# Norms and transposes of two output projections issued block by block between the units, feed-forward weight buffers swapped, and the final norm joined to each block's sums

## The chip, the cores and the metric

One core of one Trainium2 chip runs the whole program. The metric is the device time in microseconds of one execution. A core has TensorE (matmuls), VectorE (DVE), ScalarE (ACT) and GpSimd (POOL), each with a queue of its own worked off in order, and SyncE (SP), whose queue issues all the DMAs here. The engines are coupled by semaphores that the kernel writes out by hand.

## What is computed

Two transformer blocks on 1024 tokens of width 1024, in float32. The part that matters here is the end of each block:

```python
# first block
x = x + gate * (merged @ w_o)
x = rmsnorm(x, final_g)
# second block
h = rmsnorm(x, g_mix_pre);  proj = h @ w_in + b_in        # pool branch, attention branch, two gates
mix = merged @ w_out
x = x + rmsnorm(mix, g_mix_post)
h2 = rmsnorm(x, g_mlp_pre)
ff = square(relu(h2 @ w_up)) @ w_down                     # width 4096
x = x + rmsnorm(ff, g_mlp_post)
# rmsnorm(x, g) = x / sqrt(mean(x^2) + eps) * g, over the 1024 features of a token
```

## The kernel before

**Precision and units.** Every float32 operand of a projection is split into a high and a low part (`act_hi`, `act_lo`, `w_hi`, `w_lo`), and a product is three matmuls per 128 rows of depth. A unit is one PSUM bank (128 x 512) and takes 24 matmuls for a depth of 1024. `plan()` writes out one list of all units; unit number n uses bank n mod 4 (`acc`), and the semaphores `acc_ready` and `acc_free[0..3]` count units and evacuated banks, so the order of the list is the order in which TensorE and all evacuating engines work. The weights come in chunks of 8 pieces of 128 x 512: SP loads a piece into one of four `raw` slots, GpSimd casts it (L858) and subtracts (L860, `split_piece`) into one of two halves (slots) of `w_hi` and `w_lo`. A chunk's pieces may be written when the chunk two before is finished. SP's `prefetch` issues the loads of the next chunk's pieces during the current chunk's units.

**Output projections.** `wo` (first block) and `w2` (second) each have 16 units: first all eight token blocks B of the left column half (h = 0), then all eight of the right half (h = 1). VectorE evacuates each into the token-major buffer `tokT` (`evac_out`, L1459, L1461, and for `wo` an addition of x, L1465). After a block's right half ScalarE takes a mean square and a root (`mean_square_root`, L1080, L1082), VectorE scales (`norm_one`, L1470, L1471; for `w2` also the addition of the residual `x1`, L1476), ScalarE takes the mean square of that (`norm_second`), and VectorE writes the twice normed block to one of two buffers `xn` (`norm_two`, L1482, L1485). TensorE transposes it, two units of four 128 x 128 transposes per block (`turn_norm`, `turn`, L1685), named `ht` for the first block and `mt` for the second; ScalarE copies the high part out of PSUM (`split_hi`, L904) and VectorE subtracts for the low part (L1504). All turned units stand in the list behind the last unit of the projection. The next projection waits for the evacuation of the last of them, `wait_evac(pe, ("ht", 7, 1))`. What follows is `pl` (8 units) and `q` after `ht`, and the feed-forward part after `mt`.

**SP around it.** During the right half SP issues for each block the load of what is to be added (L737, L787), the store of a finished block to `x1_d` or `x2_d` (L742, L789), and the prefetches. The loads of the feed-forward weights follow behind the last two `x2_d` stores.

**Feed-forward.** The hidden width is done in NJ = 16 slices of 256. The order on TensorE is up(0), up(1), down(0), up(2), down(1), ... up(15), down(14), down(15). An `up` is 4 units of 24 matmuls (L1829), a `down` 16 units of 6 (L1842). The `up` weights lie in `w[:, 0, 0:4]`, the `down` weights in `w[:, 0, 4:8]`, the hidden activations (`hid`) in `w[:, 1]`. ScalarE takes Relu out of PSUM, VectorE multiplies by PSUM for the square, ScalarE copies the high part, VectorE subtracts. The `down` units are added into `tokT` by VectorE (L1612). GpSimd's `mlp_split(region, n0, ld, free)` waits for unit number `free` and then splits four pieces.

**End.** After the last `down`, VectorE runs `norm_one(2, B)` for the eight blocks; ScalarE's mean squares go along with the sums. SP refills the two `res` buffers with rows of `x2` (L817), each when the addition two blocks before is done, and stores the output rows (L819, L822).

Of the kernel before, what the change touches and what calls it, by code (L numbers as in the profile page):

```python
# [18 lines left out]
F32 = mybir.dt.float32  # L19
# [28 lines left out]
def plan():  # L48
# [3 lines left out]
    def chunk(key, us):  # L52
        chunks.append(key)
        units.extend(us)
        last[len(chunks) - 1] = [u for u in us if u[0] not in ("qt", "kt")][-1]
# [74 lines left out]
    chunk(("w2", 1), t_units("w2", 1))  # L130
    units.extend(("mt", B, h) for B in range(NB) for h in range(2))
# [37 lines left out]
def build(nc, A, out):  # L169
# [3 lines left out]
    M0 = len(units)  # L173
# [7 lines left out]
    with ExitStack() as ctx:  # L181
# [137 lines left out]
        rel, out_st = sem("rel"), sem("out_st")  # L319
# [127 lines left out]
        up_w = [w[:, 0, 0:4, :].rearrange("p a n -> p (a n)").rearrange("p (k n) -> p k n", k=KT)  # L447
                for w in (w_hi, w_lo)]
        down_w = [w[:, 0, 4:8, :].rearrange("p a n -> p (a n)").rearrange("p (k n) -> p k n", k=2)
                  for w in (w_hi, w_lo)]  # L450
# [33 lines left out]
        def _(sp):  # L484
# [291 lines left out]

            wait_evac(sp, ("yb", 7, 1))
# [17 lines left out]
            def mlp_pieces(src, j, before):  # L795

                for p in range(4):
                    sp.wait_ge(w_ready, before + p)
                    dst = raw[:, p, :].rearrange("p (k n) -> p k n", k=2) if src is up_src else raw[:, p, :]
                    sp.dma_start(dst, src(j, p)).then_inc(raw_ld[p], 16)  # L800

            mlp_pieces(up_src, 0, NP0 - 3)
# [24 lines left out]
        def _(pool):  # L827
# [54 lines left out]
            mlp_split(0, NP0, 0, U[chunk_last[len(chunks) - 2]] + 1)  # L882
            mlp_split(0, NP0 + 4, 1, M0 + 4)
            mlp_split(4, NP0 + 8, 2, M0 + 4)
            with pool.Fori(2, NJ) as k:

                mlp_split(0, NP0 + 8 * k - 4, 2 * k - 1, M0 + 20 * k - 32)
                mlp_split(4, NP0 + 8 * k, 2 * k, M0 + 20 * k - 16)
            mlp_split(4, NP0 + 8 * NJ - 4, 2 * NJ - 1, M0 + 20 * NJ - 16)
# [6 lines left out]
        def _(act):  # L896
# [191 lines left out]

            def normalise(r, name):
                for B in range(NB + 1):  # L1090
                    if B < NB:
                        if r == 0:
                            act.wait_ge(n_x[0], NB + B + 1)
                        else:
                            wait_evac(act, ("w2", B, 1))
                        mean_square_root(r, B, 0, n_s1[r])
                    if B >= 1:
                        norm_second(r, B - 1)
                for B in range(NB):
                    for h in range(2):  # L1100
                        wait_unit(act, (name, B, h))
                        split_hi((name, 2 * B + h), act_hi[:, 4 * h:4 * h + 4, P * B:P * B + P],
                                 bank((name, B, h)).rearrange("p (k s) -> p k s", k=4))
# [4 lines left out]
            for u in unit_range(("pl", 0, 0), ("pl", 3, 1)):  # L1108
                wait_unit(act, u)
# [34 lines left out]
            def mlp_relu(k, i, n0, before):  # L1144

                act.wait_ge(acc_ready, n0 + i + 1)
                if before is not None:
                    act.wait_ge(acc_free[i], before)
                nc.scalar.activation(relu[i], acc[i], ACT.Relu).then_inc(rel, 1)

            def mlp_hi(k, i, par, freed, down_done):
# [4 lines left out]
                nc.scalar.activation(hid[0][:, par, i // 2, HALF * (i % 2):HALF * (i % 2) + HALF], sq[i],  # L1156
# [9 lines left out]
            mlp_up(0, 0, M0, None, M4 + 1, None)  # L1166
# [12 lines left out]
        def _(dve):  # L1179
# [307 lines left out]

            def normalise(r, name):
# [3 lines left out]
                for B in range(NB + 2):  # L1492
                    if B < NB:
                        evac_out(r, B, 1, NB + B)
                    if 1 <= B <= NB:
                        norm_one(r, B - 1)
                    if 2 <= B < 4:
                        norm_two(r, B - 2)
                for B in range(NB):
                    for h in range(2):  # L1500
                        u = (name, B, h)
                        dve.wait_ge(hi_done, SPLIT[(name, 2 * B + h)])
                        cols = slice(P * B, P * B + P)
                        nc.vector.tensor_tensor(act_lo[:, 4 * h:4 * h + 4, cols],  # L1504
                                                bank(u).rearrange("p (k s) -> p k s", k=4),
                                                act_hi[:, 4 * h:4 * h + 4, cols].bitcast(F32), ALU.subtract
                                                ).then_inc(free_of(u), 1)
                    if B + 2 < NB:
# [382 lines left out]
```

## Time and profile before

| | |
|---|---|
| time, median of 3 runs | 2987.16 us |
| lowest and highest | 2985.3 and 2987.48 us |
| span of the profiled execution, core 0 | 2985.3 us, mean granted TensorE clock 0.958 |
| that execution's own time beside its span | 2985.3 us, the lowest run, agrees with the span to the digit shown; nothing is known to lie around it |
| busy: TensorE, VectorE, GpSimd, ScalarE | 93%, 46%, 30%, 21% of the span |
| DMA | 236.11 MB, mean 79 GB/s |

TensorE's two clock levels are 2.4 GHz (granted clock 1.00) and 1.2 GHz (0.50); values between are mixtures over a stretch. The chain that ended last is made of TensorE for 87% of the span, VectorE for 7%, DMA for 3%.

### The profile page before, as it was taken

To read this page: it belongs to the slowest core of one execution; us is meant where nothing else is said; L and a number is where in the kernel's file an instruction comes from. 1 tells how busy PE (TensorE), PEld (TensorE's weight loads), DVE (VectorE), ACT (ScalarE), POOL (GpSimd) and SP (SyncE) were. 2 spreads that over 40 slices of the span, in tenths; PEclk is the share of its full clock that TensorE was granted. 3 is DMA by queue.
4 is the path that set the end of the run, shared out by engine and by line. 5 is a ranking of instruction groups with operands and counts; after the bars stand their busy time and mean duration, and the time that the engine had idled before them with its cause. 6 is when DMAs were issued, how large, how long until landed. Compare 5 with 4: busy or idle time off the path is not lost.

```text
span 2985.3 us, 33951 instructions
## 1 busy us (share of the span) xinstructions
PE 2778.3 (93%) x12436; PEld 2214.1 (74%) x12436; DVE 1387.5 (46%) x2577; ACT 631.0 (21%) x1495; POOL 883.6 (30%) x862
## 2 busy tenths in 40 slices
PE   6799999999999998959898899998988999999995
PEld 2487778977799776738686777777767888888884
DVE  1411346977668675671543612224363334434435
ACT  3212222122311233440122022230141100110111
POOL 0541213323142322313343412214213433333330
PEclk8899999999999999979998999999989999999997
DMA  5410112112221222533332121214241111111112
GB/s 170 127 53 27 59 48 74 58 55 78 73 77 53 69 86 92 187 132 120 113 125 71 36 75 60 64 59 174 78 127 43 52 48 46 53 42 56 42 63 99
DMA packets 155597, 236.11 MB, mean 79 GB/s; under 512 B 24764, under 2 KB 69564, under 8 KB 155464
## 3 DMA queue, kind: packets, MB, share of 16 engines
q1 hardware_dynamic: 155464, 234.35, 24.3%
q8 instruction: 82, 1.34, 0.2%
q14 instruction: 51, 0.42, 0.0%
HBM read 181.65 MB, written 52.64 MB: 78 GB/s over the span
## 4 chain that ended last, share of the span: by engine, by line
PE 87%; DVE 7%; DMA 3%; issue 1%; POOL 1%; ACT 1%; SPq 0%; POOLq 0%; DVEq 0%; ACTq 0%
PE ps L1673 50%; PE ps L1829 12%; PE ps L1842 12%; PE ps L1731 5%; PE ps L1741 3%; PE ps L1755 3%; PE ps L1685 2%; PE ps L1702 2%; DVE act_lo L1196 1%; DVE scr L1283 1%; DMA small<-st_d 1%; DVE act_lo L1504 1%; DMA scr<-x_d 1%; POOL w_lo L860 1%; DMA scr<-in_x 0%
## 5 line engine op out<-in xcount | busy, mean ns | idle before, releaser
L858 POOL CAST w_hi<-raw 128x512 fp32r<-128x512 f32 x416 | 311.5, 749 | 2012.4 <-DMA raw<-in_w_in 932.1
L1673 PE MATMUL ps<-act_hi,w_hi 128*128 128x512 f32 x1344 | 558.2, 415 | 50.4 <-DVE act_lo L1196 46.5
L860 POOL TENSOR_TENSOR w_lo<-raw,w_hi 128x512 fp32r<-128x512 f32 x416 | 580.2, 1395 | 33.3
L1673 PE MATMUL ps<-act_lo,w_hi 128*128 128x512 f32 x1344 | 533.3, 397 | 0.0
L1673 PE MATMUL ps<-act_hi,w_lo 128*128 128x512 f32 x1344 | 531.2, 395 | 0.0
L1283 DVE SCALAR_TENSOR_TENSOR scr<-scr,small 128x512 f32<-128x512 f32 x480 | 420.6, 876 | 11.5
L1673 PE MATMUL ps<-w_hi,act_hi 128*128 128x512 f32 (+1 forms) x960 | 386.8, 403 | 6.7 <-DVE act_lo L1196 6.6
L1673 PE MATMUL ps<-w_lo,act_hi 128*128 128x512 f32 (+1 forms) x960 | 376.4, 392 | 0.0
L1673 PE MATMUL ps<-w_hi,act_lo 128*128 128x512 f32 (+1 forms) x960 | 376.3, 392 | 0.0
L1673 PEld LDWEIGHTS ps<-act_hi,w_hi 128*128 128x128 f32 x1344 | 257.2, 191 | 104.5 <-issue 56.5
L1673 PEld LDWEIGHTS ps<-act_lo,w_hi 128*128 128x128 f32 x1344 | 256.0, 190 | 57.6
L1673 PEld LDWEIGHTS ps<-act_hi,w_lo 128*128 128x128 f32 x1344 | 257.5, 192 | 45.6 <-issue 0.2
L1673 PEld LDWEIGHTS ps<-w_hi,act_hi 128*128 128x128 f32 x960 | 233.6, 243 | 31.8 <-issue 12.5
L1673 PEld LDWEIGHTS ps<-w_hi,act_lo 128*128 128x128 f32 x960 | 234.0, 244 | 20.9
L1673 PEld LDWEIGHTS ps<-w_lo,act_hi 128*128 128x128 f32 x960 | 234.6, 244 | 19.3
L1000 ACT ACTIVATE scr<-scr,stat 128x256 f32<-128x256 f32 (+1 forms) x256 | 118.6, 463 | 512.5 <-DVE stat L1306 510.8
L1612 DVE TENSOR_TENSOR big<-big,ps 128x512 f32<-128x512 f32 x240 | 161.3, 685 | 135.0 <-PE ps L1842 135.0
L1829 PE MATMUL ps<-act_hi,w_hi 128*128 128x512 f32 x512 | 201.3, 393 | 10.1 <-POOL w_lo L860 8.7
L1842 PE MATMUL ps<-w_hi 128*128 128x512 f32 x512 | 200.7, 392 | 7.9 <-POOL w_lo L860 7.9
L1829 PE MATMUL ps<-act_hi,w_lo 128*128 128x512 f32 x512 | 200.8, 392 | 0.0
L1829 PE MATMUL ps<-act_lo,w_hi 128*128 128x512 f32 x512 | 200.8, 392 | 0.0
L1842 PE MATMUL ps<-w_lo,w_hi 128*128 128x512 f32 x512 | 200.5, 392 | 0.0
(166 smaller groups left out, 3111.4 us busy)
## 6 DMA issues: line engine op xcount, KB each, us to landing
raw<-in_w_in SPq DMA_DIRECT2D x176, 256.0 KB, 3.1
raw<-in_w_up SPq DMA_DIRECT2D x64, 256.0 KB, 2.6
raw<-in_w_down SPq DMA_DIRECT2D x64, 256.0 KB, 2.6
vreg<-in_w_ada SPq DMA_DIRECT2D x48, 256.0 KB, 3.5
raw<-in_w_in SPq DMA_DIRECT2D x72, 128.0 KB, 2.2
x_d<-big SPq DMA_DIRECT2D x16, 512.0 KB, 3.0
scr<-x_d SPq DMA_DIRECT2D x16, 512.0 KB, 4.4
o_d<-scr SPq DMA_DIRECT2D x48, 128.0 KB, 2.0
```

The costliest lines, as they stand in the source:

```text
L858: pool.tensor_copy(dhi, src).then_inc(w_hi_done, 1)
L860: pool.tensor_tensor(dlo, src, dhi.bitcast(F32), ALU.subtract).then_inc(w_ready, 1)
L1000: nc.scalar.activation(prob[a % 2][:, 0:n], prob[a % 2][:, 0:n], ACT.Exp, scale=-1.0, bias=stat[:, B, h:h + 1], accum_out=stat[:, B, 8 + h ...
L1283: nc.vector.scalar_tensor_tensor(ca, u_in[:, j:j + HALF], w[:, j:j + 1], ca, ALU.mult, ALU.add).then_inc(tap, 1)
L1612: ins = nc.vector.tensor_tensor(dst, dst, acc[i % ACC], ALU.add)
L1673: ins = nc.tensor.matmul(out_, lhs, rhs, start=(m == 0), stop=(m == 3 * nk - 1))
L1685: ins = nc.tensor.transpose(bank(u)[:, P * i:P * i + P], src, ident[:, :])
L1731: nc.tensor.matmul(ps_s[a % 2][:, 0:n], qT[rows, pair, P * B:P * B + P], keys, start=True, stop=True).then_inc(scores, 1)
L1741: ins = nc.tensor.transpose(ps_t[:, P * i:P * i + P], prob[a % 2][:, P * i:P * i + P], ident[:, :])
L1755: ins = nc.tensor.matmul(ps_o[:, 0:HD], probT[a % 2][:, P * i:P * i + P], v, start=(i == 0), stop=(i == n // P - 1))
L1829: ins = nc.tensor.matmul(acc[i], up_w[b][:, k, P * t:P * t + P], act_p[a][:, k, HALF * h:HALF * h + HALF], start=(m == 0), stop=(m == 23))
L1842: ins = nc.tensor.matmul(acc[i % ACC], hid[a][:, par, k, P * B:P * B + P], down_w[b][:, k, HALF * h:HALF * h + HALF], start=(m == 0), stop ...
```

## The change

- The turned units of `ht` and `mt` move up in the list. From block 2 on, behind the right-half unit of block B stand the two turned units of block B - 2 (`normed`). Block 6 is turned after the first unit of what follows, block 7 after the second. `pl` is reordered for it: first the left token halves of two tiles with blocks 6 and 7 turned between, then the left halves of the other two, then the right halves. A left half needs only blocks 0 to 3, so the first `pl` unit waits for `("ht", 3, 1)` and the fifth for `("ht", 7, 1)`. The `mt` side does the same with up(0), whose four units become entries of the list (`up`, t, h) in the order left, left, right, right. All `up` groups take this order of tile and half.
- VectorE and ScalarE run in the order that this asks for: per block evacuate, `norm_two` of the block before, low halves of the block two before, `norm_one`; ScalarE: high halves of two blocks before, first mean square, second mean square.
- Weights: up(0) in region 0, the other `up` in region 4, `down` in region 0, except the last `down`, in region 4. Up(1) is split when `w2`'s left half is done (before: after up(0)), the last `down` after up(15) (before: after down(14)). The loads of the up(0) pieces are issued by SP at block 3 of the right half of `w2`.
- End: `mlp_last` adds the last `down` and scales block by block; the reciprocal and scaling of block B - 1 follow the two sums of block B. The addition of the residual goes to GpSimd. The loads, the stores and the two `res` buffers are as before.

```diff
@@ plan()
-    chunk(("wo", 1), t_units("wo", 1))
-    units.extend(("ht", B, h) for B in range(NB) for h in range(2))
-    chunk(("pl", 0), f_units("pl", range(4)))
+    def turned(name, B):
+        return [(name, B, h) for h in range(2)]
+    def normed(name, turns):
+        us = []
+        for B in range(NB):
+            us.append((name, B, 1))
+            us += turned(turns, B - 2) if B >= 2 else []
+        chunk((name, 1), us)
+    normed("wo", "ht")
+    chunk(("pl", 0), [("pl", 0, 0)] + turned("ht", 6) + [("pl", 1, 0)] + turned("ht", 7)
+          + [("pl", t, h) for h in range(2) for t in range(4)][2:])
...
-    chunk(("w2", 1), t_units("w2", 1))
-    units.extend(("mt", B, h) for B in range(NB) for h in range(2))
+    normed("w2", "mt")
+    units += [("up", 0, 0)] + turned("mt", 6) + [("up", 1, 0)] + turned("mt", 7) + [("up", 0, 1), ("up", 1, 1)]
@@ SP, right half of w2
+                        if B == 3:
+                            mlp_pieces(up_src, 0, NP0 - 3)
@@ GpSimd
-            mlp_split(0, NP0, 0, U[chunk_last[len(chunks) - 2]] + 1)
-            mlp_split(0, NP0 + 4, 1, M0 + 4)
-            mlp_split(4, NP0 + 8, 2, M0 + 4)
+            mlp_split(0, NP0, 0, U[chunk_last[last_chunk - 1]] + 1)
+            mlp_split(4, NP0 + 4, 1, U[chunk_last[last_chunk - 1]] + 1)
+            mlp_split(0, NP0 + 8, 2, M0 + 4)
...
-            mlp_split(4, NP0 + 8 * NJ - 4, 2 * NJ - 1, M0 + 20 * NJ - 16)
+            mlp_split(4, NP0 + 8 * NJ - 4, 2 * NJ - 1, M0 + 20 * NJ - 32)
+            for B in range(NB):
+                pool.wait_ge(n_scaled, B + 1)
+                pool.wait_ge(n_ld[2][B % 2], 16 * (B // 2 + 1))
+                pool.tensor_tensor(tokT[:, B, :], tokT[:, B, :], res[B % 2], ALU.add).then_inc(n_y[2], 1)
@@ ScalarE, normalise
                 for B in range(NB):
+                    if B >= 2:
+                        turned_hi(name, B - 2)
...
                     mean_square_root(r, B, 0, n_s1[r])
+                    norm_second(r, B)
@@ ScalarE, after normalise(1, "mt")
-            mlp_up(0, 0, M0, None, M4 + 1, None)
+            first_relu(0)
+            turned_hi("mt", 6)
+            first_relu(1)
+            turned_hi("mt", 7)
+            first_hi(0)
+            first_hi(1)
+            first_relu(2)
+            first_relu(3)
+            first_hi(2)
+            first_hi(3)
@@ VectorE, normalise
                 for B in range(NB):
                     evac_out(r, B, 0, B)
+                for B in range(NB):
+                    evac_out(r, B, 1, NB + B)
+                    if B >= 1:
+                        norm_two(r, B - 1)
+                    if B >= 2:
+                        turned_lo(name, B - 2)
+                    norm_one(r, B)
+                norm_two(r, NB - 1)
@@ VectorE, after normalise(1, "mt")
-            mlp_square(0, 0)
+            first_square(0)
+            turned_lo("mt", 6)
+            first_square(1)
+            turned_lo("mt", 7)
+            mlp_lo(0, 0, 0)
+            mlp_lo(0, 1, 0)
...
@@ VectorE, end
-            mlp_add(NJ - 1, M0 + 20 * NJ - 16, False, M4 + 5 * NJ - 4)
-            dve.wait_ge(bc_ld, 96)
-            for B in range(NB):
-                norm_one(2, B)
+            mlp_last(NJ - 1, M0 + 20 * NJ - 16, M4 + 5 * NJ - 4)
+            # in mlp_last, for B in range(NB + 1): the two sums of block B, then for block B - 1:
+                        dve.wait_ge(n_s1[2], B)
+                        link(nc.vector.reciprocal(r, r))
+                        nc.vector.scalar_tensor_tensor(tokT[:, B - 1, :], tokT[:, B - 1, :], r, bc[2][0],
++                                                       ALU.mult, ALU.mult).then_inc(n_scaled, 1)
```

## Rows read from the trace of the kernel before

**Rows 1.** The page: busy time, share of the span and instructions per engine.

```profile
PE 2778.3 (93%) x12436; PEld 2214.1 (74%) x12436; DVE 1387.5 (46%) x2577; ACT 631.0 (21%) x1495; POOL 883.6 (30%) x862
```

**Rows 2.** Stretches: length, busy time and instructions per engine, granted clock, DMA share, GB/s.

```profile
1572.30:1599.40 27.10, 13.51 (x64) 10.88 (x62) 23.74 (x34) 13.36 (x25) 18.20 (x14) 0.63 0.42 133
...
2207.50:2235.80 28.30, 13.55 (x64) 10.91 (x62) 25.10 (x35) 13.44 (x25) 10.66 (x8) 0.62 0.43 145
2235.80:2260.50 24.70, 24.61 (x96) 19.81 (x96) 3.27 (x6) 2.83 (x5) 0.00 (x0) 0.89 0.00 1
2260.50:2269.20 8.70, 0.05 (x1) 0.05 (x1) 3.05 (x3) 1.75 (x3) 8.21 (x9) 0.77 0.26 87
...
2923.50:2931.50 8.00, 0.12 (x2) 0.02 (x1) 0.69 (x1) 0.00 (x0) 7.31 (x8) 0.74 0.00 0
2931.50:2956.50 25.00, 24.93 (x96) 20.01 (x96) 10.36 (x16) 10.13 (x21) 0.00 (x0) 0.88 0.00 1
2956.50:2985.30 28.80, 0.00 (x0) 0.00 (x0) 21.32 (x25) 1.44 (x3) 0.00 (x0) 0.59 0.77 255
```

**Rows 3.** Chain of waits from 1500 us on: start, length, what.

```profile
1572.29 0.70 DVE big L1461
1573.02 0.70 DVE big L1465
...
1599.48 56.33 PE ps L1673 x240
...
2269.15 23.41 PE ps L1829 x96
...
2314.32 21.76 PE ps L1829 x96
```

**Rows 4.** Chain of waits in stage Z, turned units between projection units.

```profile
1247.27 0.87 PE ps L1685 x8
```

**Rows 5.** Stretches of stage Z, the transposes (L1685) alone: PE, PEld, clock, DMA.

```profile
1240.00:1280.00 40.00, 7.60 (x60) 6.67 (x60) 1.00 0.62 199
```

**Rows 6.** Timeline after the last w2 unit: start, length, engine, instruction, [idle before].

```profile
2207.53 0.69 DVE L1459 TENSOR_SCALAR big<-ps 128x512 f32<-128x512 f32 x1 [2.11 <-PE ps L1673]
...
2208.25 1.06 ACT L1080 ACTIVATE scr<-big 128x1024 f32<-128x1024 f32 x1 [1.32 <-DVE big L1459]
...
2209.43 0.29 ACT L1082 ACTIVATE stat<-stat,small 128x1 f32<-128x1 f32 x1
...
2210.98 1.28 DVE L1471 SCALAR_TENSOR_TENSOR big<-big,stat,vreg 128x1024 f32<-128x1024 f32 x1
...
2216.94 1.29 DVE L1485 SCALAR_TENSOR_TENSOR vreg<-big,stat,vreg 128x1024 f32<-128x1024 f32 x1
...
2218.14 1.28 DVE L1504 TENSOR_TENSOR act_lo<-ps,act_hi 128x512 fp32r<-128x512 f32 x2
...
2218.78 1.27 POOL L860 TENSOR_TENSOR w_lo<-raw,w_hi 128x512 fp32r<-128x512 f32 x1
...
2219.44 0.60 ACT L904 ACTIVATE act_hi<-ps 128x512 fp32r<-128x512 f32 x1 [2.46 <-PE ps L1685]
2219.53 1.60 DVE L1485 SCALAR_TENSOR_TENSOR scr<-big,stat,vreg 128x1024 f32<-128x1024 f32 x1
2219.99 1.61 POOL L858 CAST w_hi<-raw 128x512 fp32r<-128x512 f32 x1
```

**Rows 7.** Timeline of GpSimd at the end of `wo`.

```profile
1568.29 0.61 POOL L858 CAST w_hi<-raw 128x512 fp32r<-128x512 f32 x1 [2.77 <-DMA raw<-in_w_in]
1568.98 2.16 POOL L860 TENSOR_TENSOR w_lo<-raw,w_hi 128x512 fp32r<-128x512 f32 x1
```

**Rows 8.** Source view of L787, the loads of x1 rows under w2.

```profile
DMA to landing us min/median/max: 4.0/4.3/4.8
```

**Rows 9.** Source view of L817, the loads of x2 rows at the end.

```profile
DMA to landing us min/median/max: 3.5/5.0/5.8
```

**Rows 10.** Timeline of VectorE, its last instruction.

```profile
2981.00 1.22 DVE L1476 TENSOR_TENSOR big<-big,scr 128x1024 f32<-128x1024 f32 x1 [0.52 <-DMA scr<-x_d]
```

More of the change, by code:

```diff
@@ L54, in chunk @@
         units.extend(us)
-        last[len(chunks) - 1] = [u for u in us if u[0] not in ("qt", "kt")][-1]
+        last[len(chunks) - 1] = [u for u in us if u[0] not in ("qt", "kt", "ht", "mt")][-1]
     def f_units(name, tiles):
@@ L172, in build @@
     taps_after = tap_plan()
-    M0 = len(units)
+    M0 = len(units) - 4
     assert M0 % ACC == 0
@@ L445, in down_src, with mlp_w @@
             return w_down[bass.ds(j * FC + P * (p // 2), P), HALF * (p % 2):HALF * (p % 2) + HALF]
[L447 to L450, printed above, removed]
+        def mlp_w(region, nk):
+            return [w[:, 0, region:region + 4, :].rearrange("p a n -> p (a n)").rearrange("p (k n) -> p k n", k=nk)
+                    for w in (w_hi, w_lo)]
+        UPS = [("up", i % 2, i // 2) for i in range(4)]
         hid = [w[:, 1, :, :].rearrange("p a n -> p (a n)").rearrange("p (i t s) -> p i t s", i=2, t=2)
@@ L774, in _, with mlp_pieces @@
                 gate_load(i + 32, ("y2", 3), u, "g2p" if u[0] == "yp" else "g2a")
+            def mlp_pieces(src, j, before):
+                for p in range(4):
+                    sp.wait_ge(w_ready, before + p)
+                    dst = raw[:, p, :].rearrange("p (k n) -> p k n", k=2) if src is up_src else raw[:, p, :]
+                    sp.dma_start(dst, src(j, p)).then_inc(raw_ld[p], 16)
             wait_evac(sp, ("yb", 7, 1))
@@ L1486, in norm_two, with turned_lo @@
                                                bc[r][2 if r == 0 else 1], ALU.mult, ALU.mult).then_inc(n_xn[r], 1)
+            def turned_lo(name, B):
+                for h in range(2):
+                    u = (name, B, h)
+                    dve.wait_ge(hi_done, SPLIT[(name, 2 * B + h)])
+                    cols = slice(P * B, P * B + P)
+                    nc.vector.tensor_tensor(act_lo[:, 4 * h:4 * h + 4, cols],
+                                            bank(u).rearrange("p (k s) -> p k s", k=4),
+                                            act_hi[:, 4 * h:4 * h + 4, cols].bitcast(F32), ALU.subtract
+                                            ).then_inc(free_of(u), 1)
             def normalise(r, name):
@@ L1491, in normalise @@
                     evac_out(r, B, 0, B)
[L1492 to L1498, printed above, removed]
[L1499 to L1509 removed]
+                for B in range(NB):
+                    evac_out(r, B, 1, NB + B)
[5 more added lines that the diff above has]
+                norm_two(r, NB - 1)
             normalise(0, "ht")
+            turned_lo("ht", 6)
+            turned_lo("ht", 7)
             def pooling(t):
@@ L1816, in _, with up_unit @@
                 turn(("a2", B, 0), [yv[:, B, P * i:P * i + P] for i in range(4)])
-            for u in unit_range(("yp", 0, 0), ("w2", 7, 1)):
-                project(u)
-            turn_norm(1, "mt")
+            def up_unit(i, out_, region):
+                t, h = i % 2, i // 2
+                up_w = mlp_w(region, KT)
+                for m in range(24):
+                    k, (a, b) = m // 3, PARTS[m % 3]
+                    ins = nc.tensor.matmul(out_, up_w[b][:, k, P * t:P * t + P],
+                                           act_p[a][:, k, HALF * h:HALF * h + HALF],
+                                           start=(m == 0), stop=(m == 23))
+                ins.then_inc(acc_ready, 1)
+            for u in unit_range(("yp", 0, 0), ("up", 1, 1)):
+                if u[0] == "mt":
+                    turn_norm(1, u)
+                elif u[0] == "up":
+                    begin(u)
+                    pe.wait_ge(w_ready, NP0 + 4)
+                    wait_evac(pe, ("mt", 3 if u[2] == 0 else 7, 1))
+                    up_unit(UPS.index(u), bank(u), 0)
+                else:
+                    project(u)
             def up(bank_free, weights):
@@ L1824, in up, with down @@
                 for i in range(4):
-                    t, h = i // 2, i % 2
                     pe.wait_ge(acc_free[i], bank_free)
-                    for m in range(24):
-                        k, (a, b) = m // 3, PARTS[m % 3]
-                        ins = nc.tensor.matmul(acc[i], up_w[b][:, k, P * t:P * t + P],
-                                               act_p[a][:, k, HALF * h:HALF * h + HALF],
-                                               start=(m == 0), stop=(m == 23))
-                    ins.then_inc(acc_ready, 1)
-            def down(j, par, bank_free, weights):
+                    up_unit(i, acc[i], 4)
+            def down(j, par, bank_free, weights, region=0):
+                down_w = mlp_w(region, 2)
                 pe.wait_ge(w_ready, weights)
```

114 lines of the change are left out of this document (69 added, 45 removed).

## Prediction

> **What bounds the kernel now.** I read the page first: TensorE is busy 93% of the span [rows 1], so time is lost only where it stands still or runs at half clock. The chain of waits, cut to the two output projections and the end, shows such places, and a table of stretches gives their size [rows 2]. There are three.
>
> Place A, after the first output projection `wo`: 27.1 us in which TensorE has 64 transposes and nothing else, at a granted clock of 0.63, a mixture of its levels 1.2 and 2.4 GHz. From the last `wo` unit (evacuated at 1572.29) to the end of the 240 matmuls that follow it is 1655.8 - 1572.1 = 83.7 us [rows 3]. Place B, after `w2`: 28.3 us of the same, then the first `up` group in 24.7 us instead of the 21.76 us of a steady one, then 8.7 us in which only GpSimd works (the weights of the second `up` go where those of the first lie, so their split waits for its end), then 23.4 us for the second group. From 2207.3 to 2292.6 it is 85.2 us [rows 2, 3]. Place C, the end: 8.0 us wait for the split of the last `down` weights, 25.0 us for that `down` at clock 0.88, and 28.8 us of VectorE and DMA without one matmul. From 2923.6 to 2985.3 it is 61.7 us [rows 2]. Everything else on TensorE stays as it is.
>
> The span is 2985.30 us, and the fastest of the three runs shown is 2985.30 us, so nothing lies around the span; the median is 1.9 us above. The sum is made on the span and moved by 1.9 us.
>
> **Place A after the change.** The same 64 transposes are issued, now in sixteen turns of four between units of 24 matmuls. Stage Z of the kernel before does this already: eight transposes between two units take 0.87 us at full clock [rows 4, 5]. That makes 8 x 0.87 = 7.0 us. The 240 matmuls cost 240 x 21.76/96 = 54.4 us at full clock, against 56.33 [rows 3]. After: 61.4 us, if VectorE and ScalarE keep up. A block has 5.44 + 0.87 = 6.3 us. VectorE needs per block 1.4 to evacuate (two of 0.70 [rows 3]), 1.5 for the second scaling, 1.3 for two low halves, 1.5 for the first scaling [rows 6]: 5.7 us, and the ring of VectorE's scaling (1.5), ScalarE's mean square (1.5, from 2208.25 to 2209.72), the second scaling and the low halves is 5.8 us, under 6.3. The turns of block 7 come two units later than its data, so nothing waits. If GpSimd's splits add 0.3 to each of VectorE's three SBUF instructions, a block takes 6.6 us, and 8 x 0.3 us of lag fit into those two units. Gain 83.7 - 61.4 = 22.3 us, with 20 as the lower end. SP's queue: it issues the `x1` stores and the prefetch of the pieces for `q` in the old order, each behind a norm that comes no later than before; the `q` units are 50 us away, against 8 pieces of some 2.9 us (1.27 + 1.61 [rows 6]).
>
> **Place B after the change.** `w2` has an addition more (1.22 [rows 10]), and here the ring closes: first scaling with addition 2.7, ScalarE's mean square 1.5 (the next evacuation, 0.69, lies beside it), second scaling 1.5, low halves 1.3, together 7.0 us against 6.3 us of TensorE. The first norm of a block ends 6.9 us behind its unit at block 2 and 0.7 us later with each block: 10.4 at block 7. The mean square and the second scaling bring it to 13.5 us behind the last unit, and then VectorE has two squares and four low halves, 2 x 0.69 + 4 x 0.64 = 3.9, before it frees the last turned bank: 17.6 with the latencies. TensorE, with two turns, two `up` units and two turns more, could go on at 2 x 5.44 + 3 x 0.87 = 13.5. It waits 4.1 us. Until there it doesn't wait, since it needs of a block only what VectorE did one block before.
>
> GpSimd now splits the first `up` weights inside `w2`. The trace shows what it does to VectorE when both read SBUF: the scaling that starts 0.75 us after a split's subtraction takes 1.60 us instead of 1.29, and the cast behind it 1.61 us instead of 0.61 [rows 6, 7]. The two take turns. Eight GpSimd instructions cost VectorE nothing where they meet PSUM work, and at most 1.1 us each (a whole subtraction but its end), 8.8 us together. I take 1.5 us, near what four such meetings cost in the rows (4 x 0.3). TensorE's wait is then 5.6 us, bounds 2 and 13. The Trainium skill ("SBUF — State Buffer", SBUF: two separate sides) says that the pair of ports is an exclusive lock held for a whole instruction; the rows agree (1.27 + 1.28 without overlap), and by it the upper end would hold only if every instruction met its opposite.
>
> Weights: the first `up` pieces are loaded behind SP's block 3, and SP's wait there (the first norm of block 1) is fulfilled. They are 5 us of load and 8 to 12 us of split, done by block 6 or 7, before they are needed 7 us behind the last unit. The second ones wait on SP for the last norm and the last two `x2` stores: 10.4 + 0.9 + a load of 4 [rows 8] + a split of 7.5 (4 x 1.88) to 11.5 (4 x 2.88 [rows 6, 7]) = 23 to 27 us behind the last unit. They are needed at 17.6 + 2 x 5.44 = 28.5 us. So the 8.7 us go, at the price of a slack of 2 to 6 us only. After: 7.0 + 8 x 5.44 + 5.6 = 56.1 us; gain 85.2 - 56.1 = 29.1 us. ScalarE mixes Relu, Square, square root and Copy, between which the trace of before has no table load, so the mixing costs nothing.
>
> **Place C after the change.** The last `down` weights get the region that the last `up` has left, and are split under the `down` before: 8.0 us go, and with them the cold clock. `down` yields a block every 2.72 us. VectorE adds twice (1.3), scales (1.5), so it could do 2.9 us per block; what is new is that GpSimd adds the residual, and that two residual buffers are refilled behind it. No row shows GpSimd adding 1024 columns. The nearest is 512 columns in 1.27 us, so twice that at most, 2.5; a part of it is fixed, and I take 2.4. Its upper end is 4.3 us, twice the 2.16 us of a subtraction that met VectorE [rows 7]. The Trainium skill ("GPSIMD Engine Reference", 3.1 Elementwise) gives 4497 ns for 2048 columns; by that figure it would be about 2.3 us, and place C 0.7 us shorter. Two bounds on the cadence agree: taking turns with VectorE's scaling, 2.4 + 1.3 = 3.7 us; and the buffers, (2.4 + 4.8 + 0.1)/2 = 3.65 us with a load of 4.8 us, between the 4.3 us under `w2` and the 5.0 us of the tail [rows 8, 9]. The first addition can start 7.6 us into the `down` (four units, 5.44, an addition, a scaling). End: 7.6 + 7 x 3.65 + 2.4 + 3.1 (last addition to span end, as 2982.2 to 2985.3 [rows 10]) = 38.7 us. Gain 61.7 - 38.7 = 23.0 us. Bounds: with VectorE's cadence of 2.9 us it is 33 us and a gain of 28; with 4.3 us on GpSimd and turns of 5.4 us it is 53 us and a gain of 9. VectorE's instructions are late when GpSimd holds the port, but a `down` unit has four banks.
>
> **Sum.** 22.3 + 29.1 + 23.0 = 74.4 us: 2985.3 - 74.4 = 2910.9, moved by 1.9: 2912.8 us.
>
> **Rivals.** (1) *The end isn't won*: GpSimd's additions of 4.3 us set the cadence; 14 us less, 2927 us. For it: casts and subtractions that grew by 1.0 us in the rows; against it: they grew only when they met an SBUF instruction, once per block. Chance 0.13. (2) *VectorE falls behind in `w2`*, TensorE waits the full 13 us or more, and the second `up` weights, queued on SP behind the late norms, use up their slack: 8 to 12 us less, 2923 us. For it: the ring is already over the cadence; against it: the meetings in the rows cost 0.3. Chance 0.12. (3) *The clock falls under the mixed units.* Transposes alone ran at 0.63 in the gaps. If they pulled the clock down to 1.2 GHz under the sixteen units that have turns beside them, each would take 5.44 us more: 87 us, so 3000 us, slower than before; it decides from 14 such units on. Against it: stage Z has 60 transposes among its units at clock 1.00 [rows 5]. The Trainium skill ("TensorE: Matmul & The Clock Gate", Part 4: PE-mode transpose) states that transposes don't count as busy for the gate, which is the rule that speaks for this rival; the trace agrees for transposes alone. Chance 0.02. (4) *Better than forecast*: no meetings in `w2`, cadence of 2.9 us at the end: 85 us, 2902 us. Chance 0.12. The forecast itself, place by place within some 6 us: 0.60. That a part does nothing (weights still late) would cost 8 us and lies in the range: 0.01.
>
> Measurement tells this kernel from no change at about 0.2%, 6 us. The range of 2900 to 2930 us takes in the forecast and rivals 1, 2 and 4, and leaves out their far ends and rival 3. Faster 0.97, same 0.01, slower 0.02.
>
> **What would show it.** In the profile after: no stretch between `wo` and `pl` without matmuls, clock 0.97 or more there; between `w2` and `down` 56 us with one or two waits of TensorE for VectorE's low half of about 4 us in all, before the third `up` unit; no wait for GpSimd before the second `up` and the last `down`; GpSimd additions of 2.4 to 3.5 us, every 3.6 us, and a last chain of GpSimd, DMA load, GpSimd. Wrong would be a clock below 1 in the mixed stretches, `w_ready` waits, or additions over 4 us.

## The result, and the profile of the changed kernel

The changed kernel takes 2914.66 us (median of 4 runs, 2912.68 to 2915.22), the kernel before 2987.32 us (4 runs, 2985.3 to 2988.4): a ratio of 0.9756, 95% interval 0.9742 to 0.977. The forecast was 2912.8 us. The profiled execution took 2915.05 us with a span of 2912.9 us, so 2.15 us lie around the span. By that, the span of before (2985.30 us) belonged not to the run of 2985.3 us but to one that took some 2 us more (later runs of the same kernel show 1.8 us between the two, 2987.12 us with a span of 2985.3). The forecast said that nothing lies around the span and moved its sum by the 1.9 us between the median and the fastest run: that this is near the true distance is luck. Spans are compared with spans below, 2985.3 with 2912.9, 72.4 us apart where the forecast's sum had 74.4.

The page, part 1, after; it answers to [rows 1]:

```profile
PE 2759.7 (95%) x12436; PEld 2198.0 (75%) x12436; DVE 1386.1 (48%) x2569; ACT 627.4 (22%) x1495; POOL 897.2 (31%) x870
```

The same 12436 matmuls; TensorE is busy 18.6 us less, which is the cold clock that has gone, and the rest of the 72.4 us were gaps.

Stretches of the changed kernel, columns as in [rows 2]: place A; the mixed units of `w2`; its last two turns with two `up` units; the six `up` units behind; the last `down`; the end.

```profile
1572.30:1599.40 27.10, 27.10 (x133) 22.66 (x132) 12.31 (x19) 10.28 (x21) 13.25 (x15) 1.00 0.48 150
...
2103.00:2192.00 89.00, 88.21 (x404) 72.07 (x403) 40.74 (x55) 23.43 (x48) 25.55 (x24) 1.00 0.31 98
2192.00:2209.50 17.50, 15.05 (x73) 11.38 (x73) 14.80 (x23) 10.31 (x22) 2.65 (x4) 1.00 0.46 164
2209.50:2244.00 34.50, 34.48 (x145) 28.41 (x146) 9.20 (x11) 5.19 (x9) 14.00 (x13) 0.95 0.19 62
2875.08:2900.00 24.92, 21.93 (x97) 17.60 (x95) 21.93 (x27) 10.12 (x21) 11.96 (x5) 0.99 0.54 160
2900.00:2912.90 12.90, 0.00 (x0) 0.00 (x0) 7.37 (x7) 1.44 (x3) 7.03 (x3) 0.50 0.73 261
```

Against [rows 2]: the 27.1 us of place A that held 64 transposes at clock 0.63 now hold full work at 1.00. In place B two things are left: 17.5 us with 15.05 us of work, and a clock of 0.95 behind them. In place C only 12.9 us are left without a matmul, where it was 28.8.

**Place A**, chain of waits (start, length, what), answering to [rows 3]:

```profile
1571.79 4.54 PE ps L1748 x20
1576.33 0.87 PE ps L1760 x8
...
1589.90 43.57 PE ps L1748 x192
1633.47 0.44 PE ps L1760 x4
```

TensorE alone is on the chain, with two turns (eight transposes) in 0.87 us. The 240 matmuls end at 1633.47 instead of 1655.81: 22.3 us gained. From there to the start of `w2` the trace is 0.8 us longer than before.

**Place B**, from the last wait inside the first `w2` unit to the first `down`; before 2124.94 to 2292.56, 167.6 us. The chain after, in pieces:

```profile
2103.42 44.50 PE ps L1748 x195
...
2149.83 1.28 ACT L1100
...
2168.50 1.74 DVE vreg L1528
...
2171.54 1.49 DVE big L1514
2173.06 2.20 DVE big L1519
...
2186.46 1.30 DVE big L1514
...
2193.34 1.30 DVE big L1514
...
2208.18 1.21 DVE act_lo L1536 x2
2209.52 34.52 PE ps L1895 x144
```

It now takes 140.6 us: 27.0 gained, 29.1 forecast. (A row of the chain runs from one wait to the next, so the first one begins inside the first `w2` unit, where TensorE last waited.) From 2147.94 to 2209.52 the chain isn't TensorE's any more but the ring of VectorE and ScalarE: the first scaling (L1514) begins every 6.88 us (2186.46, 2193.34). The row of 1.28 us without a tile is a load of ScalarE's table ahead of the first square root. The last row has 144 matmuls in 34.52 us, where full clock makes 32.64.

**Place C**, from the last `down` (2875.08) to the end: 37.8 us instead of 61.7, 23.9 gained, 23.0 forecast. The chain ends as the forecast said, with an addition of GpSimd, the load of the last residual rows and GpSimd again:

```profile
2900.50 2.37 POOL big L907
...
2902.89 4.24 DMA scr<-x_d
```

That load lands at 2907.13, 0.3 us before VectorE's last scaling ends, so both hold the last addition back about equally. Timeline of the last blocks:

```profile
2900.35 1.27 DVE L1664 TENSOR_TENSOR big<-big,ps 128x512 f32<-128x512 f32 x2
2900.50 2.36 POOL L907 TENSOR_TENSOR big<-big,scr 128x1024 f32<-128x1024 f32 x1 [1.16 <-DVE big L1669]
...
2901.73 2.21 DVE L1669 SCALAR_TENSOR_TENSOR big<-big,stat,vreg 128x1024 f32<-128x1024 f32 x1
...
2904.02 2.34 POOL L907 TENSOR_TENSOR big<-big,scr 128x1024 f32<-128x1024 f32 x1 [1.16 <-DVE big L1669]
2904.05 3.39 DVE L1669 SCALAR_TENSOR_TENSOR big<-big,stat,vreg 128x1024 f32<-128x1024 f32 x1
2906.39 3.83 SPq L834 DMA_DIRECT2D out_y<-big  x2
2907.52 2.34 POOL L907 TENSOR_TENSOR big<-big,scr 128x1024 f32<-128x1024 f32 x1 [1.16 <-DVE big L1669]
```

GpSimd's additions take 2.34 us, and VectorE's scaling, 1.28 us alone, takes 2.21 and at last 3.39 us. Both of these scalings end 1.08 us behind the end of the addition that they met (2903.94 behind 2902.86, 2907.44 behind 2906.36), wherever they began. That is what taking turns looks like: nearly the whole scaling comes after the addition.

The sum: 22.3 + 27.0 + 23.9 - 0.8 = 72.4 us, the difference of the spans.

### The profile page after: what moved, and what is told of

It reads as the page before. It is cut to its first block, busy times and chain, and to the rows that moved or that the text cites. A ratio compares the mean times of both kernels' runs of the same rounds, so it can differ in the third digit from the quotient of the medians.

```text
span 2912.9 us, 33971 instructions
## 1 busy us (share of the span) xinstructions
PE 2759.7 (95%) x12436; PEld 2198.0 (75%) x12436; DVE 1386.1 (48%) x2569; ACT 627.4 (22%) x1495; POOL 897.2 (31%) x870
## 4 chain that ended last, share of the span: by engine, by line
PE 87%; DVE 8%; DMA 3%; ACT 1%; issue 1%; POOL 0%; SPq 0%; POOLq 0%; ACTq 0%; DVEq 0%
PE ps L1748 50%; PE ps L1895 12%; PE ps L1927 11%; PE ps L1806 5%; PE ps L1816 3%; PE ps L1830 3%; PE ps L1760 2%; PE ps L1777 2%; DVE act_lo L1239 1%; DVE scr L1326 1%; DMA small<-st_d 1%; DMA scr<-in_x 1%; DVE scr L1429 0%; DVE big L1669 0%; DVE big L1519 0%
## 5 line engine op out<-in xcount | busy, mean ns | idle before, releaser
L1748 PEld LDWEIGHTS ps<-w_lo,act_hi 128*128 128x128 f32 x960 | 234.4, 244 | 19.1
L1681 DVE TENSOR_TENSOR big<-big,ps 128x512 f32<-128x512 f32 x224 | 150.0, 684 | 112.5 <-PE ps L1927 112.5
```

The costliest lines, as they stand in the source:

```text
L1681: ins = nc.vector.tensor_tensor(dst, dst, acc[i % ACC], ALU.add)
L1748: ins = nc.tensor.matmul(out_, lhs, rhs, start=(m == 0), stop=(m == 3 * nk - 1))
```

## The experiments

All are the changed kernel with one edit each, except the last ones, which join several. The kernel before ran beside each group (medians 2987.79, 2988.2 and 2987.35 us); ratios are to it. What lies ahead of `w2` differs by some us from run to run with the same code (in the seven kernels that are alike up to `w2` the chain's `w2` row starts between 2100.83 and 2103.74), so effects under 4 us are read as lengths of stretches, in the one execution of each kernel that was profiled. These repeat: `changed_again`, the changed kernel once more, has 140.64 us in place B where the first had 140.62.

**1. Place A undone.** The first output projection goes back to all units and then all transposes, on every engine.

```diff
-    normed("wo", "ht")
+    chunk(("wo", 1), t_units("wo", 1))
+    units.extend(("ht", B, h) for B in range(NB) for h in range(2))
...
```

> The changed kernel with place A undone: all turned units of ht behind the last wo unit, pl in its old order, VectorE and ScalarE in the old order there; the rest as changed. Theory of the prediction (place A gives 22.3 us by itself, half of it idle time, the rest clock): 22 us slower than the changed kernel, about 2937 us. Rival (part of the gain at A is given back at the next place where TensorE waits for VectorE, the pooling or the yp load): under 18 us slower.

Measured: 2939.05 us, ratio 0.9831 [0.9815, 0.9848], span 2936.6, 23.7 us over the changed kernel's. From the last `wo` unit (1572.33) to the end of the 240 matmuls (1657.02) it is 84.7 us. Places B and C kept their lengths (140.6 and 37.9 us): the gain of place A is its own and isn't given back later. Of the 23.7 us, 1.2 are the 240 matmuls behind the gap, 57.50 us here and 56.33 in the kernel before: the clock behind the same gap wasn't quite the same.

**2. The two buffer swaps undone, one each.** GpSimd's split of the second `up` weights waits until the first `up` has been read, that of the last `down` weights until the `down` before has.

```diff
-            mlp_split(4, NP0 + 4, 1, U[chunk_last[last_chunk - 1]] + 1)
+            mlp_split(4, NP0 + 4, 1, M0 + 4)
```
```diff
-            mlp_split(4, NP0 + 8 * NJ - 4, 2 * NJ - 1, M0 + 20 * NJ - 32)
+            mlp_split(4, NP0 + 8 * NJ - 4, 2 * NJ - 1, M0 + 20 * NJ - 16)
```

> The changed kernel, but the split of the second up weights waits for the end of the first up again, though it has a region of its own. Theory: the 8.7 us wait of TensorE and about 1.7 us of half clock after it come back: 9 to 10.5 us slower than the changed kernel, about 2925 us. Rival (the region alone is worth it, or the split hides behind units): under 4 us slower.

> The changed kernel, but the split of the last down weights waits for the down before it again. Theory: 7.9 us wait and 3.2 us of half clock come back on TensorE, and since VectorE and GpSimd at the end follow TensorE only for the first blocks, the 3.2 us are partly hidden: 9 to 11 us slower, about 2925 us. Rival (the end is set by GpSimd and the loads alone, which can start early): under 5 us slower.

Measured: 2924.41 us (0.9788 [0.9772, 0.9805], span 2923.2) and 2926.04 us (0.9795 [0.9778, 0.9811], span 2923.4), 9.7 and 11.4 us over the changed kernel's median. Chain of the first:

```profile
2208.05 12.76 PE ps L1895 x48
...
2220.99 0.61 POOL w_hi L870
...
2229.47 24.83 PE ps L1895 x96
```

and of the second:

```profile
2874.63 0.04 POOLq L890
...
2881.16 1.27 POOL w_lo L872
...
2882.47 11.23 PE ps L1927 x36
```

The waits of before are back, 8.7 us and 7.8 us, and behind each TensorE loses 3.1 us more (24.83 instead of 21.76 us for 96 matmuls; 11.23 instead of 8.16 for 36): a swap is worth its wait and the clock behind it, some 11 us. In place B that makes 152.6 us, 11.9 over; the run's total shows 10.3, because its `w2` began 1.7 us earlier (2101.75 instead of 2103.42), which is within the scatter named above.

**3. The residual on VectorE.** GpSimd's eight additions at the end become eight of VectorE.

```diff
-                pool.tensor_tensor(tokT[:, B, :], tokT[:, B, :], res[B % 2], ALU.add).then_inc(n_y[2], 1)
...
+                        nc.vector.tensor_tensor(tokT[:, B - 1, :], tokT[:, B - 1, :], res[(B - 1) % 2], ALU.add
+                                                ).then_inc(n_y[2], 1)
```

> The changed kernel, but the residual at the end is added by VectorE behind its scaling, GpSimd does nothing there. Theory (in the changed kernel GpSimd's 2.4 us and VectorE's 1.2 us take turns, 3.57 us per block): VectorE alone needs two sums 1.27, scaling 1.45, addition 1.25, about 4.0 us per block, its last addition is 1.1 us shorter: 1 to 2.5 us slower than the changed kernel, about 2916.5 us. Rival (moving the addition to GpSimd was what gave the gain at the end): over 8 us slower. Second rival (the loads set the cadence in both): same within 1 us or faster.

Measured: 2913.75 us (0.9756 [0.974, 0.9772]), no change; the end takes 37.7 us instead of 37.8. A miss:

```profile
2898.04 1.29 DVE L1665 SCALAR_TENSOR_TENSOR big<-big,stat,vreg 128x1024 f32<-128x1024 f32 x1
...
2901.89 1.28 DVE L1665 SCALAR_TENSOR_TENSOR big<-big,stat,vreg 128x1024 f32<-128x1024 f32 x1
...
2904.54 1.28 DVE L1665 SCALAR_TENSOR_TENSOR big<-big,stat,vreg 128x1024 f32<-128x1024 f32 x1
2905.95 1.23 DVE L1668 TENSOR_TENSOR big<-big,scr 128x1024 f32<-128x1024 f32 x1
```

The cadence is worse as expected, 3.85 us (2898.04 to 2901.89) instead of 3.5 to 3.6. But the last scaling and addition take 1.28 + 1.23 us, where the changed kernel has 3.39 + 2.34. From the first scaling to the last it is 25.8 us instead of 22.7; from there to the end of the span 5.7 us instead of 8.9. What the blocks before lose, the last one gives back. The total is that of the expectation's second rival (the loads set the cadence), but not by its mechanism: VectorE works without a wait from 2878.8 to 2905.8, and only the last addition waits for its load, 0.1 us.

**4. VectorE adds only the last two residuals, and there are three residual buffers.** GpSimd keeps blocks 0 to 5.

```diff
-            for B in range(NB):
+            for B in range(6):
                 pool.wait_ge(n_scaled, B + 1)
-                pool.wait_ge(n_ld[2][B % 2], 16 * (B // 2 + 1))
+                pool.wait_ge(n_ld[2][B % 3], 16 * (B // 3 + 1))
...
```

> The changed kernel, but three residual buffers at the end, and VectorE adds the residual of the last two blocks. Theory (GpSimd and VectorE take turns, the loads are not what ends): VectorE's last scaling no longer waits 2 us for GpSimd, and the last addition takes 1.2 instead of 2.4 us: 1.5 to 2.5 us faster. Rival (the loads set the end): the third buffer gives 3 us or more. Second rival (the store and its 5 us set it): same within 0.5 us.

Measured: 2911.93 us (0.975 [0.9736, 0.9763]); the end takes 35.8 us, 2.0 less than the changed kernel's. And it tells which of the forecast's two bounds sets the cadence, for the loads are a block earlier here:

```profile
2892.97 2.27 DVE L1672 SCALAR_TENSOR_TENSOR big<-big,stat,vreg 128x1024 f32<-128x1024 f32 x1
...
2895.32 2.35 POOL L910 TENSOR_TENSOR big<-big,scr 128x1024 f32<-128x1024 f32 x1 [1.17 <-DVE big L1672]
...
2896.54 2.21 DVE L1672 SCALAR_TENSOR_TENSOR big<-big,stat,vreg 128x1024 f32<-128x1024 f32 x1
```

It is still 3.57 us (2892.97 to 2896.54), and the scaling again ends 1.08 us behind the addition (2898.75 behind 2897.67). GpSimd and VectorE taking turns set it; the third buffer did nothing for the cadence.

**5. The lag in `w2`: table, meetings, order.** Three edits, one each, against the 1.9 us that TensorE loses before its last `w2` unit and the 4.0 us behind it. `table_early`: a square root of one constant on ScalarE ahead of each `normalise`. `load_early`: SP issues the loads of the first `up` pieces four blocks of its loop earlier and so ahead of every wait for a norm; GpSimd splits them from 2142.3 to 2150.1, before the first scaling begins at 2151.3.

```diff
...
+            nc.scalar.activation(tiny[:, 35:36], epsc[:, 0:1], ACT.Sqrt)
             normalise(1, "mt")
```
```diff
-                        if B == 3:
-                            mlp_pieces(up_src, 0, NP0 - 3)
+                    elif B == 7:
+                        mlp_pieces(up_src, 0, NP0 - 3)
```

`ring_order`: the halves of an older block give way to the norm of the new one, on both engines.

```diff
-                    if B >= 2:
-                        turned_lo(name, B - 2)
                     norm_one(r, B)
+                    if B >= 2:
+                        turned_lo(name, B - 2)
...
```

> The changed kernel with one more square root of one column on ScalarE ahead of each normalise, so that the table load of 1.28 us lies under the left half. Theory (in w2 VectorE and ScalarE form a ring of 6.9 us per block against 6.3 us of TensorE, so every microsecond of delay at its start is paid by TensorE): 1.3 to 2.5 us faster than the changed kernel. Rival (there is slack at the start of the ring, or the loss at B is the half clock alone): same within 0.5 us.

> The changed kernel, but SP loads the first up pieces at the end of the left half of w2, so GpSimd splits them under blocks 0 and 1 instead of 2 to 4. Theory (the meetings at the SBUF ports cost VectorE 1.6 us of the ring): 1 to 2 us faster, less what blocks 0 and 1 pay. Rival (the meetings cost the same wherever they are): same within 0.5 us.

> The changed kernel, but per block ScalarE takes the first mean square before it copies the high halves, and VectorE makes norm_one before the low halves, so that these lie beside ScalarE's mean square. Theory (ring): the ring of w2 falls from 6.9 to about 6.3 us, TensorE waits only for the third up unit, about 2 us, and the half clock behind it goes: 3 to 6 us faster, about 2910 us. Rival (VectorE's sum of work of 6.2 us per block is the limit, not the ring): under 1.5 us faster.

Measured: 2913.37 us (0.9745 [0.9732, 0.9759]), 2910.8 us (0.9739 [0.9726, 0.9752]) and 2914.37 us (0.9759 [0.9746, 0.9773]). The last is a miss. As lengths in the chain, with the later kernels (in the last two the third `up` unit begins no row of its own):

| kernel | start of chain row in `w2` to third `up` unit | six `up` units | place B |
|---|---|---|---|
| changed | 106.10 | 34.52 | 140.62 |
| `changed_again` | 106.11 | 34.52 | 140.64 |
| `table_early` | 104.83 | 32.92 | 137.75 |
| `load_early` | 104.48 | 32.89 | 137.38 |
| `table_and_load` | 103.20 | 34.36 | 137.57 |
| `ring_order` | 105.23 | 34.50 | 139.73 |
| `turns_together` | - | - | 137.73 |
| `all_changes` | - | - | 134.76 |

The table load costs 1.27 us (its row has 1.28) and the meetings with GpSimd 1.62, what the rows of these instructions have over their usual length to 0.01 us. The meetings, in the changed kernel's timeline:

```profile
2168.50 1.74 DVE L1528 SCALAR_TENSOR_TENSOR vreg<-big,stat,vreg 128x1024 f32<-128x1024 f32 x1
...
2172.03 2.14 POOL L872 TENSOR_TENSOR w_lo<-raw,w_hi 128x512 fp32r<-128x512 f32 x1
2173.06 2.19 DVE L1519 TENSOR_TENSOR big<-big,scr 128x1024 f32<-128x1024 f32 x1
```

(0.46 + 0.20 + 0.97 = 1.6 us over 1.28, 1.29 and 1.23.) `ring_order` does bring VectorE ahead: its first scalings come every 6.1 us instead of 6.9. TensorE gains only 0.9 us of it. In the blocks that meet GpSimd it now waits for low halves (0.74, 0.73 and 0.29 us), and at the end the chain behind the turns of block 7, second Relu, high halves, low halves, is as long as ever: 1.8 us of wait before the third `up` unit. In number that is the expectation's rival (under 1.5 us), which held VectorE's work per block to be the limit; but from block 4 on the turns come every 6.35 us (2187.31, 2193.65, 2200.01, 2206.35), TensorE's own pace.

**6. The sums of these, and the turns of block 7 moved.** `table_and_load` has both edits. `turns_together` is `ring_order` with the last turns ahead of the second `up` unit, on all three engines:

```diff
-    units += [("up", 0, 0)] + turned("mt", 6) + [("up", 1, 0)] + turned("mt", 7) + [("up", 0, 1), ("up", 1, 1)]
+    units += [("up", 0, 0)] + turned("mt", 6) + turned("mt", 7) + [("up", 1, 0), ("up", 0, 1), ("up", 1, 1)]
...
```

`all_changes` joins all of experiments 4 to 6.

> The changed kernel itself, once more, beside the three others, so that gains of 1 to 4 us are read against runs on the same chip. Expected: 2914.7 us, between 2912.5 and 2916; from the start of w2 to the first down 140.6 us, and 34.5 us for the 144 up matmuls at its end if the half-clock stretch belongs to the 1.8 us wait of TensorE ahead of the third up unit; 32.7 us in this run would say that the stretch comes and goes with one and the same kernel, and that the full clock of the kernels with the early table or the early loads was chance.

> Square-root table loaded before block 0 of each output projection, and the first up weights loaded two blocks before w2, together. Theory that TensorE's lag in w2 is the sum of the table load (1.3 us) and of the meetings with GpSimd (1.6 us): from the start of w2 to the first down 136.5 to 137.5 us instead of 140.6, the median 3.5 us under the changed kernel's, since each alone gave 2.9 and 3.2 us, of which 1.6 each time was the half clock that can be won once. Rival, that each alone already took all the lag there is: no shorter than 137.4 us.

> The order of ring_order, and the turns of block 7 straight behind those of block 6, ahead of the second up unit, whose 5.4 us then lie over the high and low halves of block 7. Theory, that after ring_order the fixed chain behind the last turns (second Relu, high half, low half) is what holds the third up unit: its wait of 1.8 us and the half clock behind it (1.9 us) go, at the price of 1.0 us of waiting for the second scaling of block 7, which ends at 2201.9 in ring_order where the turns of block 6 end at 2200.9. From the start of w2 to the first down 137 us instead of 139.7; median 3 to 4 us under the changed kernel's. Rival, VectorE's ring is still what counts: 139.7 us or more, the wait only moves to the second up unit.

> Early table, early loads, the new order of the ring, the turns of blocks 6 and 7 together, three residual buffers at the end and VectorE adding the last two residuals. If the effects add: from the start of w2 to the first down 133 to 135 us (its floor, with nothing waiting, is 16 units and 8 turns, some 132.8), the end 35.8 us instead of 37.8, together 7.5 to 9.5 us under the changed kernel's median, some 2906 us. Rival, that they take the same 3 us each: 137 us and 35.8 us, 5 us under it.

Measured: 2915.36 us (0.9759 [0.9745, 0.9772]), 2912.34 us (0.9752 [0.9739, 0.9765]), 2912.47 us (0.9749 [0.9736, 0.9763]) and 2906.8 us (0.9732 [0.9719, 0.9746]). Table and meetings add up: 106.10 - 103.20 = 2.90 us for 1.27 + 1.62. Place B as a whole misses the 136.5 to 137.5 us expected, with 137.57, and is not shorter than with one edit alone: half clock is back in the six `up` units (34.36 us), so the total by itself would speak for the rival, and only the first column tells them apart. `turns_together` has no wait left behind its last turn, and no cold clock:

```profile
2198.82 1.30 DVE scr L1528
...
2200.16 0.66 PE ps L1760 x4
...
2201.47 38.27 PE ps L1895 x168
```

It still has 4.9 us over the floor of 132.8 us (23.1 units of 5.44 and 8 x 0.87, the rest of `w2` and two `up` groups; the "16 units" of the expectation is a slip, its sum isn't), since its lag in `w2` is untouched. `all_changes` has 2.0 us over the floor in place B and 35.8 us in place C, both as expected of effects that add; it is 8.6 us (0.3%) under the changed kernel beside it, with no overlap between their five runs each (2905.39 to 2910.01, 2913.65 to 2917.3), and the fastest version run.

## Why the prediction was right, and where it was off

**Place A** came out as forecast, 22.3 us. The turns cost 0.87 us per pair at full clock, as in stage Z [rows 4, 5], and TensorE waited nowhere. Experiment 1 gave it back. The units of `wo` with turns beside them, ahead of the stretch shown above, ran at full clock as well:

```profile
1520.00:1572.00 52.00, 52.00 (x251) 43.47 (x250) 35.80 (x50) 22.91 (x47) 17.11 (x16) 1.00 0.44 147
```

**Place B** was forecast at 56.1 us with 5.6 us of waiting; on the same count the changed kernel loses 7.8 us (140.6 - 132.8): 1.9 before its last `w2` unit, 4.0 behind it (17.5 us where 13.5 are work), and 1.9 of half clock behind that. Step by step:

- The ring: 7.0 us per block forecast, 6.88 measured. The third `up` unit starts 17.5 us behind the last `w2` unit. The forecast's 17.6 looks the same but is another count: there the last `w2` unit is on time and nothing meets GpSimd. With the 1.5 us for meetings the forecast is 19.1, and counted from where the last `w2` unit would end without waits it is 17.5 + 1.9 = 19.4. The wait of TensorE, 5.6 us forecast, is 5.9, but in two parts.
- "Until there it doesn't wait" failed. Once VectorE has lost some 3 us, TensorE reaches the turns of a block before that block's second scaling ends, and is led at VectorE's 6.9 us from block 3 on.
- Two things make that lag. The meetings with GpSimd were taken at 1.5 us and measured 1.62. The table load was taken as nothing ("the mixing costs nothing") and measured 1.27. Between the mixed instructions there is indeed none; but there is one ahead of the stage's first square root. The trace of before has it too, between two `w2` units, where nobody waited for it:

```profile
2171.33 1.28 ACT L1082 ACT_TABLE_LOAD   x1
```

[rows 6] begin 36 us behind it, and the forecast read no further back. The same work moved into the ring puts it on the path. (The Trainium skill, "ScalarE activation tables: per-element evaluation and per-set limits", What a function is on this engine, gives 1283 ns for such a load; the rows agree.) Without both, 106.1 falls to 103.2 us, 3.1 us over the work, where the forecast had 4.1 for the ring alone. That 1.0 us too much hid most of the missing 1.3 us of the table load: the sum of the waits came near by luck.
- The half clock behind a wait of 1.8 us wasn't in the sum. It is another 1.9 us, and it comes and goes (below).
- The second `up` weights were never late. GpSimd had them done at 2215.4, and then waited 7.1 us for the end of the first `up`, its next split:

```profile
2214.12 1.30 POOL L872 TENSOR_TENSOR w_lo<-raw,w_hi 128x512 fp32r<-128x512 f32 x1
2222.48 0.61 POOL L870 CAST w_hi<-raw 128x512 fp32r<-128x512 f32 x1 [7.06 <-PE ps L1895]
```

So the slack was 7 us, against 2 to 6 forecast. Experiment 2 shows what lies behind it: 8.7 us of wait.

**Place C** was forecast at 38.7 us and took 37.8, each term near its size. The first of GpSimd's eight additions:

```profile
2882.72 2.40 POOL L907 TENSOR_TENSOR big<-big,scr 128x1024 f32<-128x1024 f32 x1 [20.63 <-DVE big L1669]
```

It begins 7.6 us into the `down` (7.6 forecast), the last 24.8 us later (7 x 3.54; 7 x 3.65 forecast); that one takes 2.34 us (2.4), and the span ends 3.0 us behind it (3.1). The only term off is the cadence, by 0.8 us in seven blocks. Of the forecast's two bounds the turns at SBUF are the one that holds; with a third buffer it stays 3.57 us. That the last block's scaling takes 3.39 us wasn't foreseen; it is what made VectorE's own additions worth as much, and two of them worth 2.0 us.

**The rivals.** *The end isn't won*: refuted, the additions took 2.4 us and not 4.3. *VectorE falls behind*: half of its mechanism came, the lag that leads TensorE, but TensorE waited 5.9 us where the rival wanted 13, and the weights kept their slack. *The clock falls under the mixed units*: refuted, 1.00 in all of them, in both places. *Better*: not reached, even by `all_changes` (2906.8 us, 2902 in the rival).

**The total.** 72.4 us were gained where 74.4 were forecast. Place A came out to 0.1 us, place B gained 2.1 us less, place C 0.9 more, and 0.8 us were lost between A and B, where the forecast had nothing.

**What stays open.** Why the 1.8 us of wait ahead of the third `up` unit are followed by half clock in some kernels and not in others wasn't settled; the start of the wait and the length of the stretch without matmuls don't sort them (below). The 0.8 us between places A and B weren't followed up either; they are less than the 2.9 us by which the start of `w2` scatters with the same code.

## What to carry to other kernels

- Transposes between matmul units ran at full clock and at 0.87 us for eight, where in the gaps, among the waits of other engines, the clock was 0.62 to 0.63; what limited the mixing here was the ring of the engines that feed it. Work that ring out per block with everything in it, a table load too, and what its lag does once it passes the slack of the order: from there the table load and the meetings reached TensorE to 0.01 us here.
- A wait of TensorE costs its length and the clock behind it: the two buffer swaps were worth some 11 us each for waits of 8.7 and 7.8.
- Where GpSimd takes an elementwise step off VectorE, count both engines' SBUF time in a row, and let VectorE do the last pieces, which nothing overlaps.

## What the runs showed of the hardware

**The granted clock behind a short wait is not a matter of its length alone.** Kernels with the same 1.8 us of wait had different clocks in the 10 us behind it. Stretches of `changed_again`:

```profile
2207.00:2212.00 5.00, 3.24 (x14) 2.41 (x14) 4.99 (x7) 2.23 (x4) 4.84 (x5) 0.83 0.50 160
2212.00:2217.00 5.00, 5.00 (x19) 4.00 (x19) 0.00 (x0) 0.00 (x0) 3.58 (x4) 0.83 0.45 111
```

and of `table_early`, whose third `up` unit starts 0.4 us later:

```profile
2207.00:2212.00 5.00, 2.96 (x16) 2.29 (x17) 5.00 (x8) 2.54 (x5) 4.39 (x5) 1.00 0.56 191
2212.00:2217.00 5.00, 5.00 (x24) 4.13 (x23) 0.76 (x2) 0.60 (x1) 4.02 (x4) 1.00 0.35 110
```

A clock of 0.83 over 5 us is a mixture of the two levels, 2.4 and 1.2 GHz; the 144 matmuls behind took 34.52 us in the one and 32.92 in the other. The changed kernel repeated its 34.52 us, and so did the four kernels of experiments 1 to 4 whose code is the same there and that have these 144 matmuls in one row (34.50 to 34.52); `load_early` had 32.89 us, and `table_and_load`, with both edits, 34.36 us again. (The kernels with an edit inside `w2` have one trace each, so chance isn't excluded for them.) The moment in the span doesn't decide: third `up` units starting at 2206.95 (`residual_on_vector`) and 2207.86 (`vector_last_two`) were followed by half clock, the one of `load_early` at 2207.57 between them wasn't. Nor does the time without matmuls alone, in which only the last eight transposes run: it is 3.6 us in the changed kernel, `table_early` and `load_early` alike, 2.7 us in `ring_order`, which had 34.50 us, and 3.0 us in `turns_together`, which had full clock. So 1.6 us of the gain that either edit shows alone in place B are this clock and not what the edit took out of the ring.

**VectorE and GpSimd took turns in the meetings shown here, where both read SBUF and wrote SBUF.** A scaling of 1.28 us took 2.1 to 2.3 us where it met an addition of 2.4 us, and 3.39 us where it began 0.03 us behind one, ending 1.08 us behind it (2.34 - 0.03 + 1.08). The Trainium skill ("SBUF — State Buffer", SBUF: two separate sides) calls this an exclusive lock held for a whole instruction; these rows agree.

**GpSimd adds 128 x 1024 float32 elements in 2.34 to 2.41 us**, which the trace of before hadn't shown.
